# Inverting a unit lower triangle of 128 as two blocks of 64 and the block below them, and the grams of two heads in alternation

## The reference

```python
def gated_delta_rule_chunked(q, k, v, g, beta):
    ...
    a_mat = jnp.where(strict, jnp.einsum('bnhid,bnhjd->bnhij', k_beta, k) * decay, 0.0)
    t_mat = a_mat + jnp.eye(CHUNK, dtype=jnp.float32)
    solve = lambda rhs: lax.linalg.triangular_solve(t_mat, rhs, left_side=True, lower=True, unit_diagonal=True)
    value = solve(v * beta[..., None])
    ...
def rwkv7_recurrence(r, w, k, v, a_vec, b_vec):
    ...
    def step(st, inp):
        r_t, w_t, k_t, v_t, a_t, b_t = inp
        sa = jnp.einsum('bhvk,bhk->bhv', st, a_t)
        st = st * w_t[:, :, None, :] + sa[..., None] * b_t[:, :, None, :] + v_t[..., None] * k_t[:, :, None, :]
        return st, jnp.einsum('bhvk,bhk->bhv', st, r_t)
```

## Time and profile before

| | us |
|---|---|
| median of 3 runs | 3678.68 (3678.34 to 3685.58) |
| profiled execution | 3686.18 |
| its span in the trace | 3684.4 |
| TensorE busy, of the span | 3507.7 |
| VectorE busy | 2326.9 |
| ScalarE busy | 1605.9 |
| grams of the RWKV stage, first to last | 1262.9 to 1500.3 |
| inverses, first to last, RWKV stage | 1280 to about 1535 |
| inverses, first to last, gated delta stage | about 2549 to 2737 |

### The profile page before, as it was taken

The page is one execution under the profiler, slowest core; times in us unless marked ns, Lnnn a source line. Parts: engine busy times, 40 slices in busy tenths (PEclk is TensorE's granted clock), DMA queues, the critical chain, the costliest instruction groups (busy, mean ns, idle before and its releaser), DMA issues.

```text
span 3684.4 us, 66907 instructions
## 1 busy us (share of the span) xinstructions
PE 3507.7 (95%) x29212; PEld 3438.1 (93%) x29212; DVE 2326.9 (63%) x3683; ACT 1605.9 (44%) x2259; POOL 71.5 (2%) x65
## 2 busy tenths in 40 slices
PE   7999999999988999899999999988998999999997
PEld 7899999999988888799999999988998999999997
DVE  4656555556665688678666655587655776666555
ACT  4444444444444422145444444463333454444443
POOL 0000000000000000000000000001000000000000
PEclk9999999999998999799999999999998999999998
DMA  6455455555443211054555555542342555555664
GB/s 223 146 178 172 165 174 180 178 175 170 163 151 123 99 63 61 1 179 165 200 195 192 198 189 189 192 142 97 121 154 93 183 176 190 195 190 199 190 195 137
DMA packets 162630, 587.99 MB, mean 160 GB/s; under 512 B 18144, under 2 KB 18144, under 8 KB 161952
## 3 DMA queue, kind: packets, MB, share of 16 engines
q1 hardware_dynamic: 160848, 575.06, 46.7%
q0 software_dynamic: 1488, 8.65, 0.7%
HBM read 581.54 MB, written 2.10 MB: 158 GB/s over the span
## 4 chain that ended last, share of the span: by engine, by line
PE 55%; DVE 7%; ACT 1%; issue 1%; POOL 1%; ACTq 0%; POOLq 0%; DVEq 0%
PE bank L1881 16%; PE bank L1883 16%; PE bank L1882 16%; DVE pairs L2599 1%; PE bank L2051 1%; PE bank L2042 1%; PE bank L2060 1%; DVE xs L2715 1%; DVE xs L2713 1%; PE bank L1895 0%; PE bank L2093 0%; PE bank L1896 0%; PE bank L1897 0%; DVE xr L2603 0%; PE bank L2094 0%
## 5 line engine op out<-in xcount | busy, mean ns | idle before, releaser
L1881 PE MATMUL bank<-xr,pairs 128*128 128x256 f32 (+1 forms) x5664 | 1602.9, 283 | 57.8 <-DVE pairs L2599 46.5
L1882 PE MATMUL bank<-xr,pairs 128*128 128x256 f32 (+1 forms) x5664 | 1579.7, 279 | 0.0
L1883 PE MATMUL bank<-xr,pairs 128*128 128x256 f32 (+1 forms) x5664 | 1579.6, 279 | 0.0
L2294 ACT ACTIVATE pairs<-raw 128x1024 fp32r<-128x1024 f32 x1108 | 1144.7, 1042 | 985.9 <-PE bank L1883 873.6
L2599 DVE TENSOR_TENSOR pairs<-raw,pairs 128x1024 fp32r<-128x1024 f32 x1108 | 1311.1, 1202 | 342.6 <-ACT pairs L2294 339.9
L1881 PEld LDWEIGHTS bank<-xr,pairs 128*128 128x128 f32 x5664 | 1075.4, 190 | 71.5 <-DVE pairs L2599 53.6
L1882 PEld LDWEIGHTS bank<-xr,pairs 128*128 128x128 f32 x5664 | 1075.0, 190 | 1.8
L1883 PEld LDWEIGHTS bank<-xr,pairs 128*128 128x128 f32 x5664 | 1075.2, 190 | 0.0
L1881 PE MATMUL bank<-parts,pairs 128*128 128x256 f32 x1792 | 499.3, 279 | 3.2 <-DVE parts L2603 3.0
L1882 PE MATMUL bank<-parts,pairs 128*128 128x256 f32 x1792 | 497.3, 278 | 0.0
L1883 PE MATMUL bank<-parts,pairs 128*128 128x256 f32 x1792 | 497.3, 278 | 0.0
(11 more groups left out here) (564 smaller groups left out, 3556.2 us busy)
## 6 DMA issues: line engine op xcount, KB each, us to landing
raw<-in_w_in SPq DMA_DIRECT2D x176, 512.0 KB, 4.4
raw<-in_gate SPq DMA_DIRECT2D x176, 512.0 KB, 4.8
raw<-in_val SPq DMA_DIRECT2D x176, 512.0 KB, 4.2
raw<-in_down SPq DMA_DIRECT2D x160, 512.0 KB, 4.4
raw<-in_l_w_in SPq DMA_DIRECT2D x146, 512.0 KB, 3.7
raw<-in_w_out SPq DMA_DIRECT2D x64, 512.0 KB, 4.6
raw<-in_l_w_out SPq DMA_DIRECT2D x64, 512.0 KB, 4.1
raw<-in_v_in SPq DMA_DIRECT2D x48, 512.0 KB, 4.8
```

Source lines behind the costliest of these rows:

```text
L1881: mm(o, wh[:, q, :], rh[:, k, :], start=begin and q == 0, stop=False)
L1882: mm(o, wh[:, q, :], rl[:, k, :], start=False, stop=False)
L1883: last = mm(o, wl[:, q, :], rh[:, k, :], start=False, stop=end and q == c - 1)
L2294: e.activation(pair_of(n)[0], v3(raw_of(n), widths[n] // slices[n]), ACT.Copy).then_inc(*hi_made(n))
```

## The change

The four matrices are inverted as blocks. First the two diagonal blocks of 64 of each matrix are inverted, one above the other: partitions 0 to 63 hold the upper and 64 to 127 the lower one, so that X, its transpose T64 and P1 have 64 columns a matrix, 256 in all, in place of 512. Each former matmul of 128x128x128 becomes two of 64x64x64, one on rows and columns 0 to 63 of the array, one on 64 to 127, into the same bank. Levels 1 to 4 are otherwise as before. At level 5 the upper block of X alone is updated, and both blocks of the transpose. Level 6, the block below the diagonal, is two products without mask or add: `inv_p` with n = 6, a copy (`inv_below`), `inv_xt`, a copy (`inv_end`). X and T64 share one room, P1 and P6 another. GpSimd makes the start with four operations of 256 columns in place of two of 512, and clears the left half of XT.

The grams of a chunk's two heads become one step on TensorE, with two banks: BT of head 0, BT of head 1, KT of head 0, KT of head 1. Head 0 lies on rows 0 to 63 of the array and head 1 on rows 64 to 127. The mask multiplies are steps of their own, one `yield` later each. A lane of the RWKV stage yields six times for its grams instead of four times; `invert` yields as often as before.

The masks in the constants become smaller (NCON by 448 columns), which moves the tiles allocated behind them up to the next padding.

The diff shows what is new and its surroundings; the lines it replaces stand in the listing above.

```diff
+    ("lvl", 6 * 64), ("lvl1t", 128), ("ident2", 64), ("gmask", 512), ("nstrict", 128), ("inv", 1),
...
+    h = i[:64]
+    for n in range(6):
         s = 1 << n
+        lv.append(((h[:, None] // (2 * s)) == (h[None, :] // (2 * s))) & ((h[:, None] // s) % 2 == 1)
+                  & ((h[None, :] // s) % 2 == 0))
+    put("lvl", np.tile(np.concatenate(lv, 1), (2, 1)))
+    put("lvl1t", np.block([[lv[0].T, 0 * lv[0]], [0 * lv[0], lv[0].T]]))
+    put("ident2", np.tile(np.eye(64), (2, 1)))
...
+    def h4(ap):
+        return ap.unsqueeze(1).broadcast_to([128, 4, 64])
     def mask(n):
+        return h4(C("lvl", n * 64, n * 64 + 64))
...
+    HALVES = [(slice(0, 64), slice(0, 64)), (slice(64, 128), slice(64, 128))]
     def invert(j):
+        j.X, T64 = (v3(j.room[:, i * T:(i + 1) * T], 4) for i in range(2))
+        j.P1, j.P6 = (v3(j.proom[:, i * T:(i + 1) * T], 4) for i in range(2))
+        j.T64 = T64
         do("inv_start", j)
         yield
         do("inv_first", j)
+        for n in range(1, 6):
             yield
             bk = yield from bank()
             do("inv_p", j, n, bk)
             do("inv_mask", j, n, bk)
             banks.put(bk, (vec, "inv_mask", j.id, n))
             yield
+            bk = yield from bank()
+            do("inv_x", j, n, bk)
+            yield
+            do("inv_add", j, n, bk)
+            banks.put(bk, (vec, "inv_X", j.id, n))
+        yield
+        bk = yield from bank()
+        do("inv_p", j, 6, bk)
+        yield
+        do("inv_below", j, bk)
+        yield
+        do("inv_xt", j, bk)
+        yield
+        do("inv_end", j, bk)
+        banks.put(bk, (vec, "inv_XT", j.id, 6))
...
+            for q in range(2):
+                bks = []
+                for hh in range(2):
+                    bks.append((yield from bank()))
+                do("rk_gram", j, q, bks)
+                yield
+                for hh in range(2):
+                    do("rk_masked", j, 2 * q + hh, bks[hh])
+                    banks.put(bks[hh], (vec, "gram", c, 2 * q + hh))
+                    yield
             j.bkt = yield from bank()
             do("rk_bk_turn", j)
             banks.put(j.bkt, (act, "rk_BK", c))
             yield
+            j.MT, j.XT, j.room, j.proom = s["GM"][:, :, 0, :], s["XT"], s["room"], s["proom"]
...
         def inv_p(j, n, bk):
+            p4 = v3(bk.view[:, 0:T], 4)
             w.on(bk.after)
             w.wait_ge(*vec["inv_X", j.id, n - 1])
             for g in range(4):
+                if n < 6:
+                    for b, c in HALVES:
+                        last = mm(p4[b, g, :], j.MT[b, g, c], j.X[b, g, :], start=True, stop=True)
+                else:
+                    last = mm(p4[64:128, g, :], j.MT[0:64, g, 64:128], j.X[0:64, g, :], start=True, stop=True)
             last.then_inc(*pe("inv_p", j.id, n))
         def inv_x(j, n, bk):
+            p4, q4 = v3(bk.view[:, 0:T], 4), v3(bk.view[:, T:2 * T], 4)
             w.on(bk.after)
             w.wait_ge(*vec["inv_mask", j.id, n])
             w.wait_ge(*(vec["inv_XT", j.id, n - 1] if n > 1 else pool["inv_XT", j.id]))
             for g in range(4):
+                for b, _ in HALVES:
+                    if n < 5 or b.start == 0:
+                        last = mm(p4[b, g, :], j.T64[b, g, :], j.P1[b, g, :], start=True, stop=True)
+            if n == 5:
+                for g in range(4):
+                    for b, _ in HALVES:
+                        last = mm(q4[b, g, :], j.P1[b, g, :], j.T64[b, g, :], start=True, stop=True)
             last.then_inc(*pe("inv_x", j.id, n))
+        def inv_xt(j, bk):
+            q4 = v3(bk.view[:, T:2 * T], 4)
+            w.wait_ge(*vec["inv_below", j.id])
             for g in range(4):
+                last = mm(q4[0:64, g, :], j.P6[64:128, g, :], j.XT[64:128, g, 64:128], start=True, stop=True)
+            last.then_inc(*pe("inv_xt", j.id))
...
+        def rk_gram(j, q, bks):
+            s, qs = j.set.view, slice(q * 128, (q + 1) * 128)
+            w.on(bks[0].after)
+            w.on(bks[1].after)
             w.wait_ge(*vec["rk_KT", j.c])
+            for i, name in enumerate(("BT", "KT")):
+                for hh, bk in enumerate(bks):
+                    hp = slice(64 * hh, 64 * hh + 64)
+                    arv = s["AR"][hp, q, :, :].rearrange("p s n -> p (s n)")
+                    last = mm(bk.view[:, i * T:(i + 1) * T], s[name][hp, qs], arv, start=True, stop=True)
+            last.then_inc(*pe("gram", j.c, q))
...
+        def rk_masked(j, g, bk):
             gm = j.set.view["GM"][:, g, :, :].rearrange("p s n -> p (s n)")
+            w.wait_ge(*pe["gram", j.c, g // 2])
             e.tensor_tensor(gm, bk.view, C("gmask"), MUL).then_inc(*vec("gram", j.c, g))
         def inv_first(j):
             w.wait_ge(*pool["inv_XT", j.id])
             w.on(j.inv_after)
+            e.transpose(j.X, j.T64).then_inc(*vec("inv_X", j.id, 0))
         def inv_mask(j, n, bk):
             w.wait_ge(*pe["inv_p", j.id, n])
+            e.tensor_tensor(j.P1, v3(bk.view[:, 0:T], 4), mask(n), MUL).then_inc(*vec("inv_mask", j.id, n))
+        def inv_add(j, n, bk):
+            p4, q4 = v3(bk.view[:, 0:T], 4), v3(bk.view[:, T:2 * T], 4)
+            w.wait_ge(*pe["inv_x", j.id, n])
+            if n < 5:
+                e.tensor_tensor(j.X, p4, j.X, ADD).then_inc(*vec("inv_X", j.id, n))
+                w.wait_ge(*vec["inv_X", j.id, n])
+                e.transpose(j.T64, j.X).then_inc(*vec("inv_XT", j.id, n))
             else:
+                w.wait_ge(*pool["inv_zero", j.id])
+                e.tensor_tensor(j.X[0:64], p4[0:64], j.X[0:64], ADD)
+                for b, c in HALVES:
+                    last = e.tensor_tensor(j.XT[b, :, c], q4[b], j.T64[b], ADD)
+                last.then_inc(*vec("inv_X", j.id, n))
+        def inv_below(j, bk):
+            w.wait_ge(*pe["inv_p", j.id, 6])
+            e.tensor_copy(j.P6[64:128], v3(bk.view[:, 0:T], 4)[64:128]).then_inc(*vec("inv_below", j.id))
+        def inv_end(j, bk):
+            w.wait_ge(*pe["inv_xt", j.id])
+            e.tensor_copy(j.XT[0:64, :, 64:128], v3(bk.view[:, T:2 * T], 4)[0:64]).then_inc(*vec("inv_XT", j.id, 6))
...
         def inv_start(j):
             w.on(j.MT_ready)
             w.on(j.inv_after)
+            e.tensor_tensor(j.T64, j.MT[:, :, 0:64], h4(C("lvl1t", 0, 64)), MUL)
+            e.tensor_tensor(j.X, j.MT[:, :, 64:128], h4(C("lvl1t", 64, 128)), MUL).then_inc(*pool("inv_X0", j.id))
             w.wait_ge(*pool.now())
+            e.tensor_tensor(j.T64, j.T64, j.X, ADD).then_inc(*pool("inv_X1", j.id))
+            w.wait_ge(*pool.now())
+            e.tensor_tensor(j.T64, j.T64, h4(C("ident2")), ADD).then_inc(*pool("inv_XT", j.id))
+            e.memset(j.XT[:, :, 0:64], 0.0).then_inc(*pool("inv_zero", j.id))
```

More of the change, by code:

```diff
@@ L124, in constants @@
     lv = []
-    for n in range(7):
+    h = i[:64]
+    for n in range(6):
         s = 1 << n
-        lv.append(((i[:, None] // (2 * s)) == (i[None, :] // (2 * s))) & ((i[:, None] // s) % 2 == 1)
-                  & ((i[None, :] // s) % 2 == 0))
-    put("lvl", np.concatenate(lv, 1))
-    put("lvl1t", lv[0].T)
+        lv.append(((h[:, None] // (2 * s)) == (h[None, :] // (2 * s))) & ((h[:, None] // s) % 2 == 1)
[3 more added lines that the diff above has]
+    put("ident2", np.tile(np.eye(64), (2, 1)))
     st = (i[:, None] < i[None, :]).astype(np.float32)
@@ L920, in invert @@
         do("inv_first", j)
-        for n in range(1, 7):
+        for n in range(1, 6):
             yield
@@ L928, in invert @@
             yield
-            b1 = b2 = None
-            if n < 6:
-                b1 = yield from bank()
-                do("inv_x", j, n, b1)
-            if n > 4:
-                b2 = yield from bank()
-                do("inv_xt", j, n, b2)
-            yield
-            do("inv_add", j, n, b1, b2)
-            if b1:
-                banks.put(b1, (vec, "inv_X", j.id, n))
-            if b2:
-                banks.put(b2, (vec, "inv_XT", j.id, n))
+            bk = yield from bank()
+            do("inv_x", j, n, bk)
+            yield
+            do("inv_add", j, n, bk)
[10 more added lines that the diff above has]
+        banks.put(bk, (vec, "inv_XT", j.id, 6))
     def first():
@@ L1399, in lane @@
             banks.put(j.bkb, (vec, "bonus", c), (act, "rk_V", c))
-            for g in range(4):
-                bk = yield from bank()
-                do("rk_gram", j, g, bk)
-                banks.put(bk, (vec, "gram", c, g))
+            for q in range(2):
[3 more added lines that the diff above has]
+                do("rk_gram", j, q, bks)
                 yield
+                for hh in range(2):
+                    do("rk_masked", j, 2 * q + hh, bks[hh])
+                    banks.put(bks[hh], (vec, "gram", c, 2 * q + hh))
+                    yield
             j.bkt = yield from bank()
@@ L2041, in inv_p @@
             for g in range(4):
```

(21 more changed lines are left out.)

38 lines of the change are left out of this document (6 added, 32 removed).

## The result

The changed kernel takes 3639.2 us (median of eight runs, 3626.9 to 3668.0) against 3682.8 for the kernel before in the same comparison (eight runs, 3678.3 to 3706.8). The ratio is 0.9881, 95% interval 0.9849 to 0.9914, so some 44 us less, between 32 and 56. The lowest runs of the two, 3626.9 and 3678.3, are 51.4 us apart.

What follows compares the result with a forecast made beforehand. TensorE bounds the kernel, with VectorE also full in three-lane bursts. Gains 30 + 7.5 + 2.5 + 17 - 2 = 55 us take the profiled 3686.2 to 3631, the median 3678.7 to 3624; range 3598 to 3670.

Steps and rivals of the forecast that it cites:

- The step of one lane, 0.47 us: Inverse on TensorE: eight pairs of half-size products side by side take 0.47 us from start to start against 0.89.
- rival A: Inverse steps: the two halves take turns, a step takes 0.93 us, as much as now; 3661; chance 0.12.
- (a): VectorE in the inverse: a level for one lane takes 0.42 + 0.42 + 0.44 = 1.28 us instead of 2.07.
- (b): Three-lane inverse bursts: VectorE ends last, round from 5.81 to about 3.9 us; 10 us a burst, three bursts, 30 us.
- (c): Two lanes inverting, 1503 to 1543: a round of about 2.9 us for 4.3 to 4.6; 7.5 us gained.
- (d): Second stage's fourth lane alone between weight tiles, with the other lanes' lone steps: 2.5 us gained.
- (e): Grams on TensorE: a pair's two heads run side by side at one head's cost; 17 us gained, other end 6.
- (f): Waits and queues: gram order and extra turns 0; second bank at most 5 us; GpSimd's start covered, at most 5 us.
- The clock, "2 us": Bursts: TensorE will now wait there, and waits can bring half clock; 2 us taken off the gain.
- Rival C: Inverse bursts: TensorE's clock falls there with half the array's cells and waits; 20 us slower, 3699; chance 0.09.
- the 45 to 50: Sign of being right: the stretch from first gram to centre products, 280 us, gets shorter by 45 to 50 us.
- Rival B: Inverse bursts are bound by handovers, three-lane round nearer 4.8 us; 3646; chance 0.14.

Runs made afterwards that it cites:

- run without transposes: Changed kernel without VectorE's transposes of levels 1 to 4, that part of the computation left out; one run, 3619.9 us.
- inverse alone: Kernel before with the new inverse and the old gram functions and loop; 3651.8 us, ratio 0.9885 of the kernel before.
- grams alone: Kernel before with the new grams, masks and loop over pairs, and the old inverse; 3672.1 us, ratio 0.9987 of the kernel before.
- change, again: Changed kernel run again with no edit, two repeats: 3653.9 us (ratio 0.9882) and 3643.1 us (ratio 0.9875 of the kernel before).
- start on VectorE: Changed kernel with the inverse's start as two multiplies and an add on VectorE instead of four GpSimd operations; 3626.5 us, ratio 0.9835.
- start in three: Changed kernel with three GpSimd operations at the inverse's start instead of four; 3643.7 us (four runs), ratio 0.9866.
- start two turns earlier: Changed kernel with two more yields between the start on GpSimd and VectorE's transpose; 3630.1 us, ratio 0.9833.
- both: Changed kernel with three GpSimd operations at the inverse's start and two more yields behind them; 3625.8 us, ratio 0.9819.
- both, copies on ScalarE: Changed kernel with three-operation start, two more yields and level 6's two copies on ScalarE instead of VectorE; 3614.6 us, ratio 0.9795.
- straight order: Changed kernel with a pair's grams ordered BT and KT of head 0, then BT and KT of head 1; 3645.1 us, ratio 0.9871.
- both runs that change the order: Changed kernel with grams head by head (3645.1 us), or with each inverse step's four upper-half products before the four lower (one run, 3648.0 us).

## Why the forecast was right, and by how much it missed

**The step of one lane, 0.47 us: right.** Measured 0.463 to 0.467 back to back. The rule of the Trainium skill, TensorEngine Tiling (Array Packing), "Gotcha 1: PSUM Pressure", that different row tiles cannot use one PSUM bank at the same time, is not what this chip did: pairs of halves with one bank, on disjoint partitions, start 6 ns apart and the next pair 58 ns later at best. The measurement decides, and rival A (3661) falls. That no row showed rows and columns split at once made me give A 0.12; the column halves of the earlier trace rows were the right neighbour.

**(a) VectorE: right.** 0.410, 0.421 and 0.446 us for the 0.42, 0.42 and 0.44 taken. Halving the transpose's elements took it from 0.713 to 0.446 us, not to 0.36.

**(b), (c), (d): right in mechanism, sizes off both ways.** The round of three is 3.58 us, not 3.9, since VectorE's durations overlap a little (the nine of a round are 3.8 us in sum); VectorE is the bound as said, shown by the run without transposes. TensorE "under 80% busy" was a wrong sign: by durations, which overlap, it is busy 88% of 1404 to 1416. Stage 2, with one burst and the lone lane, gave 12 to 13.5 us where 12.5 was summed, and the inverse alone gave 26.6 us in stage 1 where two bursts and (c) have 27.5. Inside that, the terms were not so near; see the sum.

**(e) Grams: right.** 15.1 us for 17 in the run that has them alone.

**(f) "Other lanes cover it, at most 5 us": the step that failed.** GpSimd's start is four instructions of 0.72 us, 3.0 us with gaps, inside the bounds of 2.6 to 5.1 that I had, but the cover is not there. `inv_first` follows `inv_start` by one turn, in an order in which VectorE may not go past it. VectorE stands 13.9 us in stage 1, not 4.8, and TensorE waits 13.3 us, not 3.0. I had asked what hides the start on TensorE, not what the wait holds up on the engine that I had myself just made the bound. In the change a turn in a burst is half as long and the start is longer, but that is only part: the grams alone, with the old start and the old steps, already raise TensorE's wait to 8.1 us, though (f) had put their new order and the two more turns at 0. Why they do so no run shows. Three ways to take the wait away (other engine, earlier, fewer instructions) each shorten stage 1, to 257.3, 258.4 and 260.6 us from 267 to 275, and both latter together to 253.6, 55 less than before: by that the first stage gives more than forecast.

**The clock, "2 us": too small.** In stage 1 of the kernel before, TensorE was at 1.2 GHz for 36 us; after the change it is 61, 44 and 67 us. A burst shows the price: 20.5 us at 1.2 GHz instead of 3.4 make it 44.9 us instead of 37.9. What the engine did before the clock fell at 1302.0 is in the rows above: it stood 2.17 us for the start at 1301.1. But before the longest low stretch of that burst, 1325.9 to 1339.5, it had been busy for 12.4 of 13.7 us with no wait over 0.54 us, and the repeats have the same waits for the start and the long stretch elsewhere or not at all. The versions with less of the wait have 39, 34, 32, 25 and finally 17 us at 1.2 GHz in the stage, and 0 to 3.4 us in each burst. So that the waits bring the clock down is likely; that they alone do is not so. Rival C, the bursts themselves pulling the clock down, is refuted as a whole, since 1398 to 1432 ran at 0.95 and the last version's bursts at 1.00 with the same half-filled array; its sign, a clock below 0.9 in 1300 to 1460, was only just missed (0.91). The Trainium skill, TensorE: Matmul & The Clock Gate, Part 1, has activity set the clock; the runs agree in direction (fewer waits, less time at 1.2 GHz), and no run here separates the activity of half an array from the waits.

**The sum.** The prediction's own terms give 20 + 7.5 + 17 - 2 = 42.5 us for stage 1, not the 45 to 50 that it names as a sign. Measured are 33 to 42. The first gram alone comes about 3 us later after the first `lora` product in the three traces of the change and with the grams alone (31 to 32 us for 28.3 before and with the inverse alone), which (f) had allowed for the second bank; whether the bank is the reason no run shows. Where the rest went shows in three stretches: the two bursts, each from its first inverse step to the next weight product, and the last lanes, from the first inverse step of the last two to the first `center` product. Times in us, in brackets those at 1.2 GHz:

```
                           burst 1     burst 2     last lanes
grams alone                51.0 (0)    51.0 (0)    44.4 (10)
after                      44.9 (21)   37.9 (3)    40.0 (26)
change, again              38.3 (3)    37.9 (3)    40.0 (26)
change, again              38.1 (3)    44.9 (21)   40.3 (26)
start on VectorE           36.4 (0)    36.5 (0)    37.1 (21)
start in three             36.4 (3)    36.7 (3)    38.4 (21)
start two turns earlier    34.2 (0)    34.2 (0)    36.8 (19)
both                       33.7 (0)    33.7 (0)    36.2 (19)
both, copies on ScalarE    32.8 (0)    32.8 (0)    31.6 (7)
```

Against the grams alone, a burst gave 13 us where (b) has 10, even with the waits of (f) in it; 6 us where the clock fell; and the last lanes gave 4 us where (c) has 7.5, with 16 us more at 1.2 GHz. So the forecast came near in part by luck: bursts cheaper than summed offset a wait and a clock that had been priced too low. With 3.4 us at 1.2 GHz in both, the start in three instructions takes 1 to 2 us off a burst, which is the wait's own share without the clock. The start on VectorE takes off 1.4 to 1.9 us, and an estimate from the price above puts the 3.4 us at 1.2 GHz that its bursts no longer have at 1.4 us (3.4 x 7.0 / 17.1): the wait went, but its work came onto the engine that bounds the burst.

**Rival B** (handovers, 3646) is nearest in time to the median, but by its place it is wrong: the rounds are 3.6 us, not 4.8, and the loss lies at the starts and in the clock.

## What to carry to other kernels

When an engine becomes the bound of a stage, look at what stands in its order waiting for a third engine: a wait that other lanes covered before may be covered no longer, and a cheap cure is to ask for the work a few turns earlier; here that gave as much as moving the work to another engine. Small products on quarters of the array can run two at a time into one bank, if they are issued pairwise; check for starts a few ns apart. And where the whole-kernel time scatters by 1%, compare stages of the traces: over three traces of the change stage 2 repeats within 1.5 us and stage 1, where the clock moves, within 9.

## What the runs showed of the hardware that was not expected

**Two rhythms of the same stream of matmuls.** In feed-forward stages TensorE has no gaps, full granted clock, and yet the records of 256 columns start either 113.3 or 117.8 ns apart, constant for hundreds of microseconds. A stretch of 200 us in the last part, of the changed kernel's profiled execution and of its first repeat (matmuls in brackets behind TensorE's busy time, clock 1.00 in both):

```profile
3020.00:3220.00 200.00, 200.00 (x1767) 200.00 (x1767) 125.16 (x164) 92.82 (x110) 0.00 (x0) 1.00 0.59 194
```
```profile
3020.00:3220.00 200.00, 200.00 (x1700) 200.00 (x1700) 123.15 (x162) 90.38 (x107) 0.00 (x0) 1.00 0.56 186
```

200 us by 1767 are 113.2 ns, by 1700 117.6. From the end of stage 2 to the last record that makes 853.3 and 882.5 us. The first feed-forward part shows the same: between the two stages lie 967 to 970 us in ten traces and 988 to 996 in those of the straight order, the start on VectorE, the start asked for earlier and the version with both edits. The kernel before scatters too (3678 to 3690 and, less often, 3697 to 3745). The rhythm changes where the stream has a short break: in the straight order, the start asked for earlier and the version with both edits the slow one ends at a break of 1.1 us, at 2165, 2145 and 2144, while with the start on VectorE it goes on past that break. So a single time can be off by 20 to 29 us for a reason that lies outside the changed stages; what sets the rhythm is open, and whether the changed kernel meets it more often too. Times further out, such as 3745 of the kernel before, have no trace.

**A stage's order seen through the array.** In both runs that change the order, the first record of the other row half started past three waiting records of the first half, and with seven of them issued ahead it waited until three were left. A pair of heads takes 1.06 us in either order, but the last record of a lone step of sixteen starts at 0.75 instead of 0.47 us.
